# Delta-net stage: the inverse turned from its transpose, the decay turned from a broadcast copy and masked by VectorE, no drains of TensorE behind weight blocks

## The reference, cut to what matters

```
q, k, v = silu(conv(h @ w)); q, k normalised per head
g = -exp(a_log) * softplus(a + dt_bias);  beta = sigmoid(b)
G = cumsum(g)                             # within a chunk
decay = where(i >= j, exp(G_i - G_j), 0)
A = where(i > j, beta_i * (k_i . k_j) * decay, 0) + I
u = A^-1 (beta v);  w = A^-1 (beta exp(G) k)
a_qk = where(i >= j, (q_i . k_j) * decay, 0)
v_new = u - w S;  o = (q exp(G)) S + a_qk v_new
S = S * exp(G_last) + (k exp(G_last - G))^T v_new
```

## Time and profile before

| | |
|---|---|
| runs, us | 2562.07, 2562.87, 2566.28; median 2562.87 |
| the profiled execution, us | 2561.86, its span 2560.1 |
| mean granted clock of TensorE | 0.987 |
| TensorE busy, us (share) | 2493.7 (97%) |
| VectorE, ScalarE busy, us (share) | 1760.5 (69%), 1356.9 (53%) |
| the chain that ended last | PE 94%, DVE 3%, ACT 1% |
| delta-net stage | about 296 to 563 us of the span |

### The profile page before, as it was taken

How to read it: one execution, slowest core, us unless ns; L and a number is a source line. 1 busy time by engine, 2 the same in 40 slices (tenths; PEclk the granted TensorE clock), 3 DMA queues, 4 the chain that set the end, 5 groups by cost and what they waited for, 6 DMA issues and landing times.

```text
span 2560.1 us, 33508 instructions
## 1 busy us (share of the span) xinstructions
PE 2493.7 (97%) x12232; PEld 2047.0 (80%) x12232; DVE 1760.5 (69%) x1848; ACT 1356.9 (53%) x1381; POOL 9.3 (0%) x6
## 2 busy tenths in 40 slices
PE   8999999989999999999999998999999999999999
PEld 6688889757888888888888887888768878876887
DVE  6565653337888889898988887654855666547665
ACT  3544322236777777777777777443154454422544
POOL 0000000010000000000000000000000000000000
PEclk9999999998999999999999999999999999999999
DMA  7296121037999999999999996952346567523553
GB/s 283 90 320 187 58 84 67 33 107 278 374 336 381 338 374 344 355 355 357 359 355 366 347 374 210 308 181 90 124 148 194 183 210 242 180 67 130 170 186 128
DMA packets 313183, 593.55 MB, mean 232 GB/s; under 512 B 8864, under 2 KB 132896, under 8 KB 312864
## 3 DMA queue, kind: packets, MB, share of 16 engines
q1 hardware_dynamic: 313120, 592.70, 66.2%
HBM read 591.62 MB, written 1.05 MB: 232 GB/s over the span
## 4 chain that ended last, share of the span: by engine, by line
PE 94%; DVE 3%; ACT 1%; issue 1%; DVEq 1%; DMA 0%; ACTq 0%
PE bank L512 16%; PE bank L186 16%; PE bank L188 16%; PE bank L187 16%; PE bank L513 8%; PE bank L2280 4%; PE bank L1215 3%; PE bank L2314 2%; PE bank L1879 1%; PE bank L1399 1%; PE bank L905 1%; PE bank L1230 1%; PE bank L2290 1%; PE bank L1902 1%; PE bank L1313 1%; PE bank L1328 1%
## 5 line engine op out<-in xcount | busy, mean ns | idle before, releaser
L2125 DVE TENSOR_TENSOR weights_lo<-mslot,weights_hi 128x2048 fp32r<-128x2048 f32 x336 | 767.3, 2290 | 124.0 <-ACT weights_hi L2017 122.9
L2017 ACT ACTIVATE weights_hi<-mslot 128x2048 fp32r<-128x2048 f32 x336 | 644.1, 1920 | 238.1 <-PE bank L188 238.1
L512 PE MATMUL bank<-x_parts,weights_hi 128*128 128x512 f32 x1760 | 626.2, 400 | 6.0 <-DVE x_parts L363 6.0
L619 DVE TENSOR_TENSOR weights_lo<-scratch,weights_hi 128x2048 fp32r<-128x2048 f32 x165 | 377.5, 2289 | 218.6 <-ACT weights_hi L612 218.1
L513 PE MATMUL bank<-x_parts,weights_lo 128*128 128x256 f32 x1760 | 495.1, 281 | 0.0
L512 PEld LDWEIGHTS bank<-x_parts,weights_hi 128*128 128x128 f32 x1760 | 332.1, 189 | 89.1 <-DVE weights_lo L619 3.9
L186 PE MATMUL bank<-weights_hi,x_parts 128*128 128x512 f32 x944 | 374.5, 397 | 3.7 <-DVE x_parts L696 1.9
L188 PE MATMUL bank<-weights_hi,x_parts 128*128 128x512 f32 x944 | 368.7, 391 | 0.0
L187 PE MATMUL bank<-weights_lo,x_parts 128*128 128x512 f32 x944 | 368.6, 390 | 0.0
L612 ACT ACTIVATE weights_hi<-scratch 128x2048 fp32r<-128x2048 f32 x165 | 315.2, 1912 | 93.3 <-PE bank L188 93.3
L513 PEld LDWEIGHTS bank<-x_parts,weights_lo 128*128 128x128 f32 x1760 | 334.0, 190 | 1.8
(11 more groups left out here) (369 smaller groups left out, 2128.6 us busy)
## 6 DMA issues: line engine op xcount, KB each, us to landing
mslot<-in_o_moe_w_gate SPq DMA_DIRECT2D x112, 1024.0 KB, 5.6
mslot<-in_o_moe_w_up SPq DMA_DIRECT2D x112, 1024.0 KB, 5.9
mslot<-in_o_moe_w_down SPq DMA_DIRECT2D x112, 1024.0 KB, 5.8
scratch<-in_ffn_w_gate SPq DMA_DIRECT2D x44, 1024.0 KB, 5.3
scratch<-in_ffn_w_up SPq DMA_DIRECT2D x44, 1024.0 KB, 5.4
scratch<-in_ffn_w_down SPq DMA_DIRECT2D x44, 1024.0 KB, 5.0
mslot<-in_o_w_in SPq DMA_DIRECT2D x8, 2048.0 KB, 9.2
mslot<-in_w_in SPq DMA_DIRECT2D x10, 1536.0 KB, 8.7
```

The lines of the kernel that those rows point to most:

```text
L512: pe.matmul(m.ps[bank + j][:, :], hi[:, k, cols], both, start=(k == 0), stop=False)
L619: dve.tensor_tensor(m.wlo[to][:, :], m.fslot[i], m.whi[to][:, :], ALU.subtract).then_inc(m.sig["f_lo"], 1)
L2017: act.activation(m.whi[(place + half) % PLACES][:, :], r.slot[slot + half], ACT.Copy).then_inc(s["r_hi"], 1)
L2125: dve.tensor_tensor(m.wlo[i][:, :], r.slot[slot + half], m.whi[i][:, :], ALU.subtract).then_inc(s["r_lo"], 1)
```

## The change

1. Decay. VectorE broadcasts the sums `G` (not g) behind the K0 convolution, and TensorE only turns each copy (16 transposes). Nothing is masked before the exponential; VectorE takes min(dec, 1) times the strict triangle for `LT`, and in steps 13 and 17 min(dec, 1) times the full triangle in place. `qdT` comes from banks 4 and 5, where the turned copies of t = 1 lie.
2. Inverse. `update` makes TT alone. New `turn_inverse(i)` waits for ScalarE's copy of TT (`d_TT`), turns it into bank 3, and ScalarE copies it to T (`turned`). It stands one step behind its update. Level 0 is made with one VectorE instruction less, since the mask for it is prepared once, and the SiLU of V1 stands behind the four level-0 copies of ScalarE.
3. No drains on TensorE: a block's `m_used` now comes from a drain on VectorE when the convolution of its second projection has seen the filled bank, and from one on ScalarE behind the SiLU of gates 2 and 3.
4. The semaphore of the last gain is shared with that of the first ones.

The SiLU of V1 moved behind the third and fourth copy, and T's copy (L1480 on either side) waits for the turn now. The diff, cut to its core:

```diff
@@ -1216,8 +1216,6 @@
                 last.then_inc(filled(m, name), 1)
-                if n % 2 == 1:
-                    pe.drain().then_inc(s[f"m_used{i % 4}"], 1)
 
@@ -1231,8 +1229,6 @@
             last.then_inc(s[f"d_fill{n % 2}"], 1)
-            if t == 1:
-                pe.drain().then_inc(s[f"m_used{i % 4}"], 1)
 
@@ -1263,13 +1259,8 @@
         for h in range(GH):
-            pe.matmul(at(2 + 2 * t + h // 4, h), o.gb[t][:, h, :], c["upto"], start=True, stop=False)
-            last = pe.matmul(at(2 + 2 * t + h // 4, h), c["ident"], c["future"], start=False, stop=True)
+            last = pe.transpose(at(2 + 2 * t + h // 4, h), o.gb[t][:, h, :], c["ident"])
         last.then_inc(s["d_Gb"], 1)
-    pe.wait_ge(s["d_Gs"], 1)
-    for h in range(GH):
-        last = pe.matmul(at(6 + h // 4, h), o.gb[1][:, h, :], c["upto"], start=True, stop=True)
-    last.then_inc(s["d_Gb"], 1)
     project("K3")
@@ -1319,14 +1310,18 @@
             pe.wait_ge(s["d_TT"], i - 3)
-        if k < NLEV - 1:
-            if i:
-                pe.wait_ge(s["d_T"], i)
-            for h in heads:
-                pe.matmul(at(3, h), o.TT[t][:, h, :], o.Y[a][:, h % 4, :], start=True, stop=True)
         for h in heads:
             last = pe.matmul(at(4 + a, h), o.Y[a][:, h % 4, :], o.TT[t][:, h, :], start=True, stop=True)
         last.then_inc(s["d_Z"], 1)
+
+    def turn_inverse(i):
+        t, heads = group(i % 4)
+        pe.wait_ge(s["d_TT"], i + 1)
+        if i:
+            pe.wait_ge(s["d_T"], i)
+        for h in heads:
+            last = pe.transpose(at(3, h), o.TT[t][:, h, :], c["ident"])
+        last.then_inc(s["d_Tp"], 1)
 
@@ -1337,6 +1332,8 @@
             update(i - 1)
+        if 2 <= i < NSTEP - 2:
+            turn_inverse(i - 2)
         if i % 2 == 0 and i < 20:
@@ -1457,9 +1454,8 @@
         last.then_inc(s["d_dec"], 1)
-    act.wait_ge(s["d_Gb"], 3)
     for g in range(2):
-        last = act.activation(o.qdT[:, 4 * g:4 * g + 4, :], heads4(m.ps[6 + g]), ACT.Exp)
+        last = act.activation(o.qdT[:, 4 * g:4 * g + 4, :], heads4(m.ps[4 + g]), ACT.Exp)
     last.then_inc(s["d_dec"], 1)
@@ -1467,30 +1463,35 @@
     for a in range(2 * NT):
-        if a == 2:
-            silu("V1")
         act.wait_ge(s["d_T0p"], a + 1)
         act.activation(o.T[a // 2][:, a % 2 * 4:a % 2 * 4 + 4, :], heads4(m.ps[2 + a % 2]),
                        ACT.Copy).then_inc(s["d_T0a"], 1)
+    silu("V1")
 
     def inverse(i):
         a = i % 4
         act.wait_ge(s["d_Z"], i + 1)
-        if i < NSTEP - 4:
-            act.activation(o.T[a // 2][:, a % 2 * 4:a % 2 * 4 + 4, :], heads4(m.ps[3]),
-                           ACT.Copy).then_inc(s["d_T"], 1)
         act.activation(o.TT[a // 2][:, a % 2 * 4:a % 2 * 4 + 4, :], heads4(m.ps[4 + a]),
                        ACT.Copy).then_inc(s["d_TT"], 1)
+
+    def turned(i):
+        a = i % 4
+        act.wait_ge(s["d_Tp"], i + 1)
+        act.activation(o.T[a // 2][:, a % 2 * 4:a % 2 * 4 + 4, :], heads4(m.ps[3]), ACT.Copy).then_inc(s["d_T"], 1)
 
     def gate(n):
         ring_full(act, m, f"G{n}")
         t, half = n // 2, n % 2
         act.activation(o.sg[:, t, half * HALF:(half + 1) * HALF], m.ps[n % 2][:, :],
                        ACT.Silu).then_inc(released(m, f"G{n}"), 1)
+        if t == 1:
+            act.drain().then_inc(s[f"m_used{(B_ODD + 6 + half) % 4}"], 1)
 
     for i in range(NSTEP):
         if i:
             inverse(i - 1)
+        if 2 <= i < NSTEP - 2:
+            turned(i - 2)
         if i % 4 == 2 and i < 22:
@@ -1551,8 +1552,11 @@
         x, raw, w = taps(name)
+        n = PROJECTED.index(name)
         if 0 in parts:
             ring_full(dve, m, name)
+            if n % 2 == 1:
+                dve.drain().then_inc(s[f"m_used{(B_ODD + n // 2) % 4}"], 1)
         for j in parts:
@@ -1567,6 +1571,7 @@
     dve.tensor_tensor(levels, levels, bc(c["ident"], 1, NLEV - 1), ALU.add)
+    dve.tensor_tensor(c["level"][:, 0:P], c["ident"], c["level"][:, 0:P], ALU.subtract)
     dve.wait_ge(s["d_ab"], 1)
@@ -1581,9 +1586,6 @@
     dve.scalar_tensor_tensor(v["g"], v["ea"], -1.0, v["sp"], ALU.mult, ALU.mult).then_inc(s["d_g"], 1)
-    dve.drain()
-    for t in range(NT):
-        dve.tensor_copy(o.gb[t], bc(th("g", t), 2, P)).then_inc(s["d_gb"], 1)
 
@@ -1592,11 +1594,14 @@
     dve.drain().then_inc(s["d_Gs"], 1)
+    for t in range(NT):
+        dve.tensor_copy(o.gb[t], bc(o.G[:, t * GH:(t + 1) * GH], 2, P)).then_inc(s["d_gb"], 1)
     conv("K1")
     conv("K2")
     for t in range(NT):
         dve.wait_ge(s["d_dec"], t + 1)
-        dve.tensor_tensor(o.LT[t], o.dec[t], bc(c["before"], 1, GH), ALU.mult)
+
+        dve.scalar_tensor_tensor(o.LT[t], o.dec[t], 1.0, bc(c["before"], 1, GH), ALU.min, ALU.mult)
     conv("K3")
@@ -1621,12 +1626,11 @@
         dve.drain()
-        dve.tensor_tensor(o.TT[t][:, four(g), :], o.LT[t][:, four(g), :], bc(c["level"][:, 0:P], 1, 4), ALU.mult)
-        dve.drain()
-        dve.tensor_tensor(o.TT[t][:, four(g), :], bc(c["ident"], 1, 4), o.TT[t][:, four(g), :],
-                          ALU.subtract).then_inc(s["d_T0"], 1)
         dve.tensor_tensor(o.LT[t][:, four(g), :], o.LT[t][:, four(g), :], bc(c["ident"], 1, 4),
                           ALU.add).then_inc(s["d_L"], 1)
+        dve.drain()
+        dve.tensor_tensor(o.TT[t][:, four(g), :], o.LT[t][:, four(g), :], bc(c["level"][:, 0:P], 1, 4),
+                          ALU.mult).then_inc(s["d_T0"], 1)
 
@@ -1658,6 +1662,9 @@
             values(i // 4 - 2)
+        elif i in (13, 17):
+            dec = o.dec[i // 4 - 3]
+            dve.scalar_tensor_tensor(dec, dec, 1.0, bc(c["upto"], 1, GH), ALU.min, ALU.mult)
         elif i % 4 == 0 and i < 24:
...
```

More of the change, by code:

```diff
@@ L336, in final_scale @@
         dve.drain()
-        dve.wait_ge(s["final_in"], 16)
+        dve.wait_ge(s["gains_in"], 32)
     dve.scalar_tensor_tensor(m.xn[:, t, at:end], m.res[:, t, at:end], m.rstd[t], final_gain(m)[:, at:end],
@@ L2553, in _ @@
             sp.wait_ge(s["f_h"], 5 * NU)
-            sp.dma_start(final_gain(m), w["final"]).then_inc(s["final_in"], 16)
+            sp.dma_start(final_gain(m), w["final"]).then_inc(s["gains_in"], 16)
             to = out[0].rearrange("(t p) d -> p t d", p=P)
```

## The result

The changed kernel takes 2544.77 us (median of 4 runs, 2542.61 to 2545.32), the kernel before 2564.57 beside it: ratio 0.9923, 95% interval 0.9911 to 0.9934. That is 19.8 us less where 26.05 were forecast, and 1.3 us outside the range. Most of the gain came by the mechanism forecast; the size is off by 6 us. Against the time forecast, 2536.8, the result is 8.0 us too long: 6.3 from the smaller gain and 1.7 because the kernel before, now with a fourth run, has a median of 2564.57 in place of 2562.87.

The account below looks back on a forecast made before the run. TensorE, busy nearly the whole span, was taken to bound the kernel. Terms of -11.99, -2.41, -9.10, -0.75, -1.26 and -0.54 summed to -26.05 us from 2561.86, giving 2535.8, or 2536.8 as a median; range 2533 to 2543.5.

Parts of the forecast that it names:

- decay block: Between K2 and K3, 16 transposes replace 40 matmuls, 1.75 us in place of 8.93: -7.18 us.
- inverse, with its small waits: Inverse steps: a transpose replaces T's product in 20 steps, -9.10 us; small waits go too, -0.75.
- drains of TensorE (eight): Drains leave TensorE: K1 and K3 -0.84 us, V3, Q1 and Q3 -1.26, two gate blocks -0.54.
- large wait and groups of VectorE: Before the first inverse step: wait shrinks from 4.32 to 0.85 us, -3.47; shorter VectorE groups remove another wait, -0.50.
- low clock behind the wait: Behind the large wait the clock stays full instead of 0.50: 0.98 + 1.43, -2.41 us.
- the closest point, one microsecond of slack before V3: V1's convolution on VectorE ends at 362.1 us; TensorE asks for its bank at 363.09, for V3's first half.
- (1): The wait before the first inverse step stays, as V1's convolution or the copies are late: 2542.7 us, 11%.
- (2): In the inverse, the two-copy way of T stalls; all 20 steps lose their 0.455 us again: 2545.9 us, 5%.
- (3): In the inverse, transposes are no cheaper than products; 9.10 + 1.8 us gone: 2547.7 us, 2%.
- (5): The stage shortens but the expert stage starts no earlier, for a weight block released late: about 2562 us, 3%.
- (4): TensorE's clock falls to its lower level inside the inverse, with transposes in every step: 2603 us, slower, 3%.
- Unknown is how the low clock falls elsewhere: +-2 us: Elsewhere, as from 563 to 600 us, where the clock rises may move when all comes 26 us earlier: +-2 us.

Follow-up runs that it names:

- `before_kept_busy`: Kernel before with square sums 128 columns wide, 16-column matmuls made 80 wide, and seven dummy matmuls per norm but the first: 2558.79 us, ratio 0.9979.
- `after_kept_busy`: Changed kernel with square sums 128 columns wide, 16-column matmuls made 80 wide, and seven dummy matmuls per norm but the first: 2533.28 us, ratio 0.9882.
- the filled pair: Kernel before and changed kernel, both with the widened matmuls and the dummy matmuls at the norms: 2558.79 and 2533.28 us.
- `filled_silu_back`: `after_kept_busy` with V1's SiLU back between the second and the third copy on ScalarE: 2534.82 us (2531.94 to 2537.78).
- `decay_only`: Kernel before with the decay block of the change alone: 2559.69 us, ratio 0.9981 (0.9968 to 0.9994).

## Why the prediction was right in kind and wrong in size

Each term against the clean stage, that is, TensorE's start-to-start times of `before_kept_busy` less those of `after_kept_busy`, and against the runs that undo one. The last row is the difference of the whole stage; the terms above it come to the same within 0.1:

| term | forecast | clean profiles | undone on the chip |
|---|---|---|---|
| decay block | 7.18 | 7.18 | 7.0 |
| inverse, with its small waits | 9.85 | 9.95 | 10.2 |
| drains of TensorE (eight) | 2.64 and V1's | 3.5 | 3.2 |
| large wait and groups of VectorE | 3.97 less V1's drain | 3.7 | 1.5 for the order alone |
| low clock behind the wait | 2.41 | 2.8 | not by itself |
| sum | 26.05 | 27.2 | 25.5 (the filled pair, all of the change) |

- **Decay block, inverse:** right, to 0.1 us in the profile. The broadcast copies, the masks with a minimum and the second copy of the inverse stay hidden, as argued; the closest point, one microsecond of slack before V3, held: TensorE has no wait before V3.
- **Drains:** 0.42 was taken from one start to the next. Gate blocks came to 0.37 each instead of 0.27, because the matmul behind a drain is also longer: 2.05 in the row at 511.38 of the earlier trace rows, 1.95 for the same form at 484.30 above.
- **Large wait:** the amount was right, the reason only half. The forecast ascribed it to the SiLU's place, which by `filled_silu_back` is 1.5 us of it. Which part of the change brought the full clock behind the wait isn't shown.
- **Rivals.** (1), (2), (3) and (5) didn't occur: waits, copies, transposes and weight blocks are as forecast. Rival (1)'s 2542.7 lies near the result by accident: the wait that it keeps is gone. (4) didn't either: 368 to 460 us has a clock of 1.00 with four transposes in nearly every step, and 327 to 330 us with 16 in a row. The Trainium skill (TensorE: Matmul & The Clock Gate, PE-mode transpose) says that the full clock doesn't engage for a transpose; these windows don't bear that out for transposes among matmuls, and the measurement decides.
- **The step that failed** is "Unknown is how the low clock falls elsewhere: +-2 us", with its base: one profile of the kernel before, nearly free of spells, and a median of three runs. By the filled kernels the spells cost the kernel before 2564.38 - 2558.79 = 5.6 us in the median (29 and 12 runs), and the changed kernel 2544.77 - 2533.28 = 11.5 and, run again, 2541.87 - 2533.28 = 8.6. By the ratios these are 5.4, 10.5 and 8.7. The filled versions also lack the spells behind norms, so these are sums over all places. The difference, 3 to 6 us, is what was missing. In the profiled pair it is 9.4 us: 2.7 ahead of the stage, where both kernels have the same code, 5.5 in it and 1.3 behind. Nearly all of the 5.5 can be named: the three spells of the changed kernel cost 1.7, 1.6 and 3.3 us, the one of the kernel before 1.6, and the low clock behind its large wait was 0.4 milder than in the filled one.

What makes the spells cost more after the change is shown in one place only, the 1.7 us that the large wait used to swallow. The rest, 1 to 4 us, is open. It may hang on where the narrow stretches fall in time, or partly on which executions happened to be taken; no run here sets that place at will, and the runs that moved the stage don't settle it. What VectorE's shorter chain gives alone, without the new order on ScalarE and without the other terms, wasn't tried either.

## What to carry to other kernels

A sum of start-to-start differences on the bounding engine was right to 1 us in 26; the total was off because the narrow-matmul stretches have low-clock spells that come in some runs only. List these places before forecasting, look at more than one profile of the kernel before, and widen the range by what a spell costs at each: here nothing, about 1.7 or about 3.3 us; and when a wait is removed, ask what it had been hiding. To measure a small term, first fill such places so that the clock stays up, then undo one term at a time: the runs of `decay_only` spread over 14 us, those of the filled kernels over 1 to 6, mostly under 4.

## What the runs showed of the hardware

- Widening 32 matmuls of float32 from 1 to 128 columns cost 0.08 us in all (3.49 to 3.57), and the low clock that followed them in 13 of 20 places followed in none of 16. Widening others from 16 to 80 columns and adding seven dummy matmuls per norm took, with the wide sums, 5.6 us off the kernel before, though all three add work.
- A stretch in which TensorE was busy without a gap (7.00 of 7.00 us, 476 to 483) ran at a granted clock of 0.51, with narrow matmuls at its start and ahead of it.
- Sixteen transposes in a row, between projections, ran at a clock of 1.00 and took 0.11 us each (327.37 to 329.12).
- The clock behind a wait of TensorE was 0.50 after 4.16 us in the kernel before and full after 2.26 us in `filled_silu_back`; but in `decay_only` 2.02 us were followed by a half projection of 5.14 us in place of 3.46, with a spell some 20 us ahead of it. So the length of the wait alone didn't decide it here.
